# Norm statistics as columns, the convolution's norm inside the last heads, the output projection entered among them, two projection tiles opened side by side, and buffers placed at multiples of 128 bytes

## The reference

```python
for l in range(DEPTH):                                 # DEPTH = 2
    h = _rmsnorm(x, g_mix[l])                          # norm 0
    p = h @ w_in[l]
    c_q  = _rmsnorm(p[..., :384], g_q[l])              # norm 2
    c_kv = _rmsnorm(p[..., 384:640], g_kv[l])          # norm 1
    ...                                                # q, k, v of 8 heads, rotary parts
    y_attn = _mla_attention(q_nope, q_rope, k_nope, k_rope, v)
    a, gt = jnp.split(p[..., 672:], 2, axis=-1)
    u = _dwconv(a * jax.nn.sigmoid(gt), w_dw_conv[l], b_dw_conv[l])      # 31 taps, 512 channels
    u = jax.nn.silu(_layernorm(u, g_conv_ln[l], b_conv_ln[l]))           # norm 3
    x = x + jnp.concatenate([y_attn, u], axis=-1) @ w_o[l]
    h2 = _rmsnorm(x, g_ffn[l])                         # norm 4
    ...                                                # feed-forward
return _rmsnorm(x, g_final)
```

## Time and profile before

| what | value |
| --- | --- |
| median of three executions | 3025.68 us (3022.63 to 3028.54) |
| the profiled execution | 3028.47 us |
| its span, first to last instruction | 3026.7 us |
| mean granted TensorE clock | 0.965 of 2.4 GHz |
| busy: TensorE, VectorE, ScalarE, GpSimd | 93%, 59%, 26%, 58% |
| first mixer layer; second mixer layer | about 15 to 312 us; 675 to 957 us |
| second block | from about 1331 us |

### The profile page before, as it was taken

One profiled execution on the slowest core, in us unless ns is written; L12 is line 12 of the kernel. 1 busy time (PEld: TensorE's weight loads), 2 busy tenths in 40 slices (PEclk: granted clock), 3 DMA queues, 4 the chain that ended last, 5 costly groups with the idle time before them and its releaser, 6 DMA issues.

```text
span 3026.7 us, 35770 instructions
## 1 busy us (share of the span) xinstructions
PE 2827.2 (93%) x12832; PEld 2291.1 (76%) x12832; DVE 1775.7 (59%) x1941; ACT 777.0 (26%) x1256; POOL 1764.7 (58%) x1000
## 2 busy tenths in 40 slices
PE   6898899999787999989999989999999998899998
PEld 5676788887676888877776778888777777788876
DVE  8884566428855666256656557054666665842644
ACT  2332222102423222023555312011222221310202
POOL 5983566667944766654443447666553343566663
PEclk9998999999998999999999989999999998899999
DMA  3111222232011322322111113222221111232221
GB/s 134 56 43 49 77 97 97 99 104 91 28 36 55 110 95 95 106 79 73 63 63 56 63 65 108 93 95 97 77 90 62 56 56 50 76 99 96 97 98 49
DMA packets 66367, 237.36 MB, mean 78 GB/s; under 512 B 7152, under 2 KB 7408, under 8 KB 66224
## 3 DMA queue, kind: packets, MB, share of 16 engines
q1 hardware_dynamic: 65392, 234.00, 23.2%
q10 hardware_dynamic: 832, 1.51, 0.2%
HBM read 233.38 MB, written 2.10 MB: 78 GB/s over the span
## 4 chain that ended last, share of the span: by engine, by line
PE 77%; DVE 12%; DVEq 5%; issue 3%; ACT 2%; DMA 0%; ACTq 0%; SPq 0%
PE ps L457 23%; PE ps L463 22%; PE ps L460 22%; PE ps L1013 2%; PE ps L579 1%; DVE ps L1594 1%; DVE qw L2224 1%; PE ps L802 1%; DVEq L2226 1%; PE ps L1049 1%; PE ps L805 1%; DVE rstd L1567 1%; DVE ssum L1498 1%; DVE ssum L2072 0%; DVE x_lo L1486 0%
## 5 line engine op out<-in xcount | busy, mean ns | idle before, releaser
L398 POOL TENSOR_SCALAR w_hi<-w_raw 128x1024 fp32r<-128x1024 f32 x437 | 481.2, 1101 | 1193.3 <-PE ps L457 1182.5
L400 POOL TENSOR_TENSOR w_lo<-w_raw,w_hi 128x1024 fp32r<-128x1024 f32 x437 | 1108.8, 2537 | 36.4
L457 PE MATMUL ps<-x_hi,w_hi 128*128 128x512 f32 x2024 | 817.9, 404 | 74.1 <-DVE x_lo L2110 16.3
L463 PE MATMUL ps<-x_hi,w_lo 128*128 128x512 f32 x2024 | 797.8, 394 | 0.0
L460 PE MATMUL ps<-x_lo,w_hi 128*128 128x512 f32 x2024 | 797.8, 394 | 0.0
L457 PEld LDWEIGHTS ps<-x_hi,w_hi 128*128 128x128 f32 x2024 | 386.0, 191 | 177.0 <-issue 33.8
L460 PEld LDWEIGHTS ps<-x_lo,w_hi 128*128 128x128 f32 x2024 | 386.7, 191 | 83.5 <-issue 5.5
L463 PEld LDWEIGHTS ps<-x_hi,w_lo 128*128 128x128 f32 x2024 | 385.9, 191 | 82.9
L457 PE MATMUL ps<-a_hi,w_hi 128*128 128x512 f32 x512 | 201.8, 394 | 0.0
L463 PE MATMUL ps<-a_hi,w_lo 128*128 128x512 f32 x512 | 201.0, 393 | 0.0
L460 PE MATMUL ps<-a_lo,w_hi 128*128 128x512 f32 x512 | 199.2, 389 | 0.0
(11 more groups left out here) (377 smaller groups left out, 4566.6 us busy)
## 6 DMA issues: line engine op xcount, KB each, us to landing
w_raw<-wts SPq DMA_DIRECT2D x437, 512.0 KB, 3.3
xres<-xT SPq DMA_DIRECT2D x2, 1024.0 KB, 8.8
outT<-xres SPq DMA_DIRECT2D x1, 2048.0 KB, 7.1
pf<-pT ACTq DMA_DIRECT2D x2, 512.0 KB, 3.5
prm<-prm SPq DMA_DIRECT2D x1, 452.0 KB, 3.9
lev<-levels ACTq DMA_DIRECT2D x1, 384.0 KB, 3.1
wtmp<-pos SPq DMA_DIRECT2D x1, 128.0 KB, 3.1
ident<-identity SPq DMA_DIRECT2D x1, 64.0 KB, 10.6
```

The source lines that it names most:

```text
L398: nc.gpsimd.tensor_scalar(w_hi[:, s, :], w_raw[:, s, :], 1.0, 0.0, ALU.mult, ALU.add).then_inc(w_rounded[s], 1)
L400: nc.gpsimd.tensor_tensor(w_lo[:, s, :], w_raw[:, s, :], w_hi[:, s, :].bitcast(F32), ALU.subtract).then_inc(w_split[s], 1)
L457: mm = nc.tensor.matmul(out, whi, xhi, start=first, stop=False)
L463: return nc.tensor.matmul(out, wlo, xhi, start=False, stop=last)
```

## The change

1. **Norms in columns.** `row_stat` multiplies each 128x128 piece of the sum (as the stationary side) by a single column of ones, so the sums lie as 128 tokens by 4 columns. Root and reciprocal work on 128x4 (`rowm`). `row_factor` spreads the four columns again over 128 partitions with four products against the identity, into `ps[4]` or `ps[7]`, from where VectorE reads the factor. For norm 0 ScalarE copies it to `rstd`.
2. **Norms 1 and 2 without `rstd`.** ScalarE evacuates the five kv and q tiles itself, with the gain, and squares them from PSUM (`taken`). The missing division is undone by an epsilon that is scaled by the sum of squares of x (`ecol`, `ebias`; x's own sum now lies in `root`).
3. **Opening side by side.** `IN_STEPS` takes tiles 0 and 1 of the input projection alternately. The `row_stat` of norm 0 moves from behind tile 0 to behind kt = 4 of tile 2, its `row_factor` to before kt = 2 of tile 3. In the first layer GpSimd waits, before it splits block 2, until all of x is split.
4. **Convolution.** GpSimd takes channel tile 2 instead of 1, with `POOL_TAPS` {15: 3, 17: 4, 19: 24} instead of {10: 1, 11: 1, 12: 1, 13: 1, 15: 2, 17: 10, 18: 8, 19: 7}. VectorE's steps are placed anew: 45 instead of 39 before the keys.
5. **Key banks** [2, 3, 5, 1] instead of [2, 3, 0, 1], and output banks [1, 2, 3, 4, 0, 5, 1, 2].
6. **Last heads.** The sum of the four convolution tiles is made inside head 6, between the row maxima of the last head; the norm's sums, squares, root and scaling lie beside the last head; the output projection's first block begins before `weighted` of the last head (`mixed`).
7. **Places.** `ones_r`, `big` and `yconv` are moved so that every large buffer starts at a multiple of 128 bytes. Before, the buffers from `big` on started 64 bytes behind one (`f_hi`, `a_hi`, `xg_hi`, `y2_hi`, `k_hi`), those from `yconv` on 32 bytes (`u_hi`, `cq_hi`, `kv_hi`, `q_hi`). `x_hi`, `x_lo` and the weight ring were at a multiple of 128 already.
8. **Output** as eight DMAs, one behind each tile.

```diff
+IN_STEPS = ([(0, 0), (0, 1), (0, 2), (1, 0), (1, 1), (0, 3), (1, 2), (1, 3)]
+            + [(t, kt) for kt in range(4, KD) for t in (0, 1)] + [(t, kt) for t in range(2, W_IN) for kt in range(KD)])
...
+        top[0] = (top[0] + 127) // 128 * 128
         big = top[0]
...
-            sp.wait_ge(out_ready, KD)
-            sp.dma_start(out.rearrange("(t p) s -> p t s", p=P), xres[:, :, :]).then_inc(s_out, 16)
+            for m in range(KD):
+                sp.wait_ge(out_ready, m + 1)
+                sp.dma_start(x_out[:, m, :], xres[:, m, :]).then_inc(s_out, 16)
...
+                    if l == 0 and n == 2:
+                        pool.wait_ge(x_split, KD)
                     split(l * LBLK + n)
...
+            def row_stat(out, l, k, extra=None):
+                pe.wait_ge(sum_ready, l * 6 + (k + 1))
+                for tt in range(TT):
+                    c = slice(tt * P, (tt + 1) * P)
+                    mm = nc.tensor.matmul(out[:, tt:tt + 1], (root if k <= 0 else ssum)[:, c], ones[:, 0:1], start=True,
+                                          stop=extra is None)
+                    if extra is not None:
+                        mm = nc.tensor.matmul(out[:, tt:tt + 1], root[:, c], ecol[:, extra, :], start=False, stop=True)
+                mm.then_inc(stat_ready, 1)
+            def row_factor(out, n):
+                pe.wait_ge(root_used, n + 2)
+                for tt in range(TT):
+                    mm = nc.tensor.matmul(out[:, tt * P:(tt + 1) * P], rowm[:, 1, tt:tt + 1].to_broadcast([P, P]), ident[:, :],
+                                          start=True, stop=True)
+                mm.then_inc(factor_ready, 1)
...
+                last, wo = HEADS - 1, {}
+                stat(ps[6][:, :], l, 3)
+                for kt in range(TT):
+                    if kt == 0:
+                        weighted(last - 1, 0)
+                    scores(last, kt)
+                    if kt:
+                        weighted(last - 1, kt)
+                    if kt == 1:
+                        turned(last // 2 - 1)
+                wo[0] = block_in((lb, O_WO))
+                mixed(0, [0], [0, 1])
+                for qt in range(TT):
+                    weighted(last, qt)
+                row_stat(ps[7], l, 4)
+                mixed(0, [0], [2])
+                mixed(0, [1], [0, 1, 2])
+                row_factor(ps[7], l * 5 + 3)
+                turned(HEADS // 2 - 1)
...
+                for h in range(HEADS - 1):
+                    for qt in range(TT):
+                        if h == HEADS - 2 and qt == 2:
+                            conv(PER * 3)
+                            dve.drain()
+                            dve.wait_ge(stat_ready, l * 6 + 3)
+                            V.tensor_tensor(ssum[:, :], yconv[:, 0, :], yconv[:, 1, :], ALU.add)
+                        row_max(h + 1, qt)
+                        conv(1)
...
+                        if h == HEADS - 2 and qt == 2:
+                            dve.drain()
+                            V.tensor_tensor(ssum[:, :], ssum[:, :], yconv[:, 3, :], ALU.add)
+                            dve.drain()
+                            dve.wait_ge(pconv_done, l + 1)
+                            V.tensor_tensor(ssum[:, :], ssum[:, :], yconv[:, POOL_CH, :], ALU.add).then_inc(sum_ready, 1)
```

More of the change, by code:

```diff
@@ L479, in _ @@
                       + [b for b in W_O_BANK if b < 4] + [m % 4 for m in range(KD + 2 * FT)]):
                 BU[n] += 1
-            pe.wait_ge(s_id, 16)
             with pe.Fori(0, DEPTH) as l:
                 lb = l * (LBLK // R)
-                for t in range(W_IN):
+                entered = {}
+                for t, kt in IN_STEPS:
                     b = t % 4
[L488 to L492, removed]
-                        mm = three(ps[b][:, :], w_hi[:, s, kt * P:(kt + 1) * P], w_lo[:, s, kt * P:(kt + 1) * P],
-                                   x_hi[:, kt, :], x_lo[:, kt, :], kt == 0, kt == KD - 1)
+                    if kt == 0:
+                        bank(b, l * BU[b] + 1)
+                        entered[t] = block_in((lb, t))
+                    s = entered[t]
+                    if t < 2:
+                        pe.wait_ge(x_split, l * 2 * KD + (kt + 1))
+                    if t == 3 and kt == 2:
+                        pe.wait_ge(s_id, 16)
+                        row_factor(ps[4], l * 5)
+                    mm = three(ps[b][:, :], w_hi[:, s, kt * P:(kt + 1) * P], w_lo[:, s, kt * P:(kt + 1) * P],
+                               x_hi[:, kt, :], x_lo[:, kt, :], kt == 0, kt == KD - 1)
+                    if t == 2 and kt == 4:
+                        row_stat(ps[4], l, 0)
+                    if kt < KD - 1:
+                        continue
@@ L619, in _, with mixed @@
                             turned(h // 2 - 1)
-                    if h + 1 < HEADS:
-                        max_row(h + 1)
+                    max_row(h + 1)
                     if h + 2 < HEADS:
                         query(h + 2)
-                for qt in range(TT):
-                    weighted(HEADS - 1, qt)
-                turned(HEADS // 2 - 1)
-                for n, (half, m0) in enumerate(W_O_ORDER):
-                    s = block_in((lb, O_WO + n))
-                    ring = range(3) if n == 0 else range(4)
-                    for m, kts in [(m0, ring), (m0 + 1, ring)] + ([(m0, range(3, 4)), (m0 + 1, range(3, 4))] if n == 0 else []):
+                def mixed(n, ms, kts):
+                    half, m0 = W_O_ORDER[n]
+                    for m in ms:
                         b = W_O_BANK[m]
@@ L1487, in split_x, with add_square @@
                                        ALU.subtract).then_inc(x_split, 1)
-            def add_square(i, last, n, sums):
+            def add_square(i, last, n, sums, acc=ssum):
                 dve.drain()
@@ L1627, in _ @@
                 gate_a(1, 2)
-                conv(7)
+                conv(6)
                 gate_g(1, 3)
@@ L1795, in _, with residual @@
                                     ALU.subtract).then_inc(u_split, 1)
-                def residual(m, b, index, n, gain, sqn, sums):
+                def residual(m, b, index, n, gain, sqn, sums, total=ssum):
                     acc(index)
```

286 lines of the change are left out of this document (144 added, 142 removed).

## The result

The kernel after takes 2977.91 us (median of 4, 2976.41 to 2978.90), the one before 3027.11 (median of 4, 3022.63 to 3030.95): the ratio is 0.984, 95% interval [0.983, 0.986]. The prediction was 2977.5, in a range of 2948 to 2999. The total is right.

What follows compares the result with a forecast made beforehand. TensorE, busy 93%, bounds the kernel: time goes only where it waits, runs at 1.2 GHz or has slow products. 9.5 + 29 + 5.8 + 4.0 = 48.3 off 3028.5 gives 2980.2, 2.8 lower as median: 2977.5 us, range 2948 to 2999.

Steps and rivals of the forecast that it cites:

- Step 1: Large buffers at multiples of 128 bytes: their products take x's pace, saving 9.5 us (bounds 0 and 14).
- Step 2: Mixer opening: VectorE's evacuations start about 8 us later in the second layer; the first layer ends up like it.
- Step 3: Input projection: VectorE's saved work pays the opening back, about 3.5 us ahead when the heads begin (bounds 0 and 11).
- 2 ahead at the keys: VectorE in the input projection: net 10 us saved against 8 lost in the opening.
- Step 4: Head 6: VectorE waits some 3 us for GpSimd's channel, ending at 862.9; last head's lead is about 1.
- Step 5: Last head's scores to sum behind output projection: 67.3 us for 80.8; with the lead 14.5 a layer, 29 together.
- a sign of failure: Mixer tails: the forecast fails if drops to 1.2 GHz take over 12 us of each tail, or none.
- Step 6: Norm 4 and the final norm: 1.9 us saved twice and 2.0 at the end, 5.8 in all (2 to 7).
- Step 7: Output: the last piece of 256 KB lands in 3.1 to 3.9 us, saving 4.0 us (0 to 4.5).
- GpSimd is in time: Head 6: no stall for GpSimd's channel and no clock drop; up to 12 us a layer more, about 2957; chance 0.25.
- Two drops or an opening not paid back: Mixers: two full clock drops per tail, or VectorE's opening not repaid; 8 us a layer less, 2993; chance 0.13.
- Slower: Head 6: GpSimd's channel ends later, using up the gain at 24 us a layer; about 3047 if taps block; chance 0.03.

Runs made afterwards that it cites:

- experiment 1: Kernel before with only the buffer places changed to multiples of 128 bytes: 3015.87 us, ratio to before 0.9966.
- experiment 2: Kernel after with 32 bytes put ahead of its large buffers, u and yconv rounded up again: 2999.02 us, ratio to before 0.9910.
- experiment 7: Kernel after with input projection tiles 0 and 1 one after the other: 2975.20 us, ratio to before 0.9831.
- experiment 3: Kernel after with norm 0's row sums and factor spread five steps earlier: 2966.38 us, ratio to before 0.9800.
- experiment 4: Kernel after with VectorE's wait for GpSimd's channel and the convolution's mean moved later: 2968.55 us, ratio to before 0.9811.
- experiment 6: Kernel after with the output projection's first nine groups moved out of the last head to behind it: 2990.51 us, ratio to before 0.9885.
- experiment 9: Experiment 8's kernel with twelve more output projection products ahead of the last head's weighting, the spread later: 2960.06 us, ratio to before 0.9776.
- experiment 10: Experiment 8's kernel with GpSimd splitting block 16 ahead of its first three taps: 2957.86 us, ratio to before 0.9765.
- experiment 12: Kernel after with the edits of experiments 3, 4, 9, 10 and 11 together: 2965.57 us, ratio to before 0.9794.
- experiment 8: Kernel after with the edits of experiments 3 and 4 together: 2959.75 us, ratio to before 0.9790.
- experiment 11: Experiment 8's kernel without GpSimd's wait for the low halves of x in layer 1: 2961.84 us, ratio to before 0.9784.

## Why the prediction was right, and where it was not

**Step 1, places.** Right. 9.5 predicted, 10 to 11 measured alone (experiment 1). The mechanism holds in both directions (experiment 2). The Trainium skill (SBUF — State Buffer, Operand start alignment) asks for a multiple of the element size as a matter of legality and says that its runs timed nothing. Taken as a rule of speed it would have left this part at 0; the traces do not agree with that.

**Step 2, opening.** The lateness was right: 17.2 us behind the last addition in layer 2, as given. In layer 1 the sum comes 3.3 us later (34.0 before, 37.3 now, 4 predicted), by the two effects that were named: the low halves take 10.3 us for 16.0, the seven additions 14.1 for 5.4. The first evacuation comes 5.2 later, so this layer is better off than the second; the prediction made them equal. Between the first product and the first query it gained 6.9 us where layer 2 gained 1.3. Side by side does nothing for it (experiment 7). The trace shows one difference: in layer 1 TensorE stands for the sum in both kernels, before with 24 products done, now with 63, so that its 64th product starts 24.0 us behind the first and not 30.5. That this makes the 6.9 is not shown; experiment 3 puts the 64th back to 29.8, and its mixer is 3.0 us shorter all the same. The 0.2 us for the small reciprocal was read from records of TensorE, which say nothing of VectorE; that it took 0.18 is luck.

**Step 3, pay-back.** This step failed. "2 ahead at the keys" sums up VectorE's time and forgets when TensorE asks for it. At tile 6 VectorE is still behind; TensorE stands 3.7 us there and loses 4.45 more at the lower clock; the 14 tiles end at 92.0 us and not at 80.2. At the first query the lead is 1.3 us in layer 2, not 3.5. Experiment 3 starts the evacuations 3.6 us earlier and gains 11.5 us. By the end of head 6, just ahead of the stall of step 4, the lead of layer 2 has grown to 3.5 (186.8 against 190.3 behind the first product), so the price of this step is paid in the tiles, and of VectorE's lateness 1 us is left at the last head (step 4).

**Step 4, GpSimd's channel.** The mechanism was right and named in its place: VectorE stands in head 6, the last row maximum behind it, TensorE idle. The size was off, 7.7 for 3. Counted from the layer's first product the channel was to end at 187.3 and ended at 192.3: it began 3.3 later (86.7 for 83.4, the late opening again) and took 105.6 for 103.9. VectorE was at its wait at 185.4, predicted 184.4. The lead of 1 us at the last head became a lag of 6.3: the 7.7 us, and the products behind them at the lower clock until 852. Experiment 4 removes this stall; experiment 3 shows that an earlier norm does not.

**Step 5, tail.** Right in kind and too small. From the last head's first scores to the sum: 80.8 before, 60.0 after, where 67.3 was predicted, with 60.3 for the work alone. The 7 us for drops of the clock did not come; the only drop lies in the stall ahead of the head and just behind it, 1.6 us of it in this stretch (850.4 to 852). The prediction had named this as a sign of failure (drops over 12 us in each tail, or none), so its account of the clock here was wrong and only the waits were right. Experiment 6 gives a part of the reason: take the projection's products out of the head and the waits and the lower clock are back, 6.9 us in this layer. The other 14 of the 20.8 gained were not tested by a run that puts the norm back behind the head; for them stands the trace, in which TensorE is busy for 60.8 of 63.4 us. The error of step 4 and that of step 5 are of nearly one size, 7.3 each: layer 2 gained 14.5 up to the sum, to the tenth what was predicted, by luck (and with the 0.85 in it that step 1 had counted by itself). Layer 1 gained 20.4, by its better opening: 6.9 at the first query, where layer 2 had 1.3.

**Step 6, norms.** From the sum to the first product behind norm 4: 9.0 before, 8.2 in layer 2 and 7.4 in layer 1 after, so 0.8 and 1.6 and not 1.9 each. In layer 2 both sums and spread run at 1.2 GHz (the window's 0.50; 1.87 and 2.07 us), in layer 1 the spread alone (sums 1.05), and this is the 0.8 between the layers. The final norm gave the 1.9 (from the start of the last product ahead to that of the first behind, 11.6 and 9.7). 4.3 in all for 5.8.

**Step 7, output.** 5.0 for 4.0. The last piece of 256 KB lands in 2.0 us, not in the 3.1 of a smaller transfer at the start. Here the fixed cost of about 2 us in the Trainium skill (DMA: Bandwidth & Descriptors, Anatomy of one DMA — SWDGE (gpsimd) path) was nearer than the row I chose. It is fitted there to transfers that GpSimd issues, and these go by SyncE's queue; with the time for the data that stands beside it, 256 KB would take 2.6 us, an estimate, more than the 2.0 measured.

**The sum.** In span: mixers to the sum 20.4 + 14.5, norms 4.3, output 5.0, and outside the mixers 6.5 (feed-forward 1.2 + 1.5, second block 3.7): 50.7 of 50.8. These are stages of the same two traces, so that they must add up. That the 6.5 are the places is read from experiment 1, which gained 5.5 in these stages; its other 4.7 lay in the mixers (3.8 and 0.9), where step 1 had 1.7, within what one execution's stages are good to. The median was given as 2977.5 where the sum makes 2977.4.

**The rivals.** "GpSimd is in time" did not happen. "Two drops or an opening not paid back" happened in half: in the tiles of layer 2 the opening was not paid back, the drops in the tail stayed out. "Slower" was GpSimd's channel, and it was 5 late, not 24, and no run varied its end alone, so the price of one microsecond a layer is not shown. (The 34.6 of this rival should be 24 x 1.4 = 33.6; its chance does not hang on it.)

## What to carry to other kernels

A sum of an engine's saved time says nothing about when its results are asked for: put its own timeline against each place where the bound engine waits for it. A wait in a queue blocks all that stands behind it; ask what could be done first, and move it there (experiment 4), but expect the next dependency right behind the one you took away (experiments 9, 10 and 12). Where two chains start from the same point, an earlier start of both changes nothing between them (experiment 3); what is left to change is their lengths, or the place of the wait.

## What the runs showed of the hardware that I had not expected

- Moving 32 bytes changes the pace of products with 512 columns by 3%: 0.2267 us with the moving operand's tile at a multiple of 128 bytes, 0.229 at 64 behind one, 0.2335 at 32 behind one (experiments 1 and 2). The tiles a and f, 2592 products of the kernel, were moved. No run moved the weights or x.
- A wait of 3.7 us cost 8.1: 8.9 us at half the clock followed it (kernel after), and both went together (experiment 3). The 32 narrow products of `weighted` did not bring the clock down by themselves (1.00 in the window of the kernel after), with waits around them it stood at 0.77 (experiment 6).
- VectorE's addition of 0.69 us takes up to 2.6 beside GpSimd's splits, since it ends just behind the split (experiment 8). A gate that keeps GpSimd away from one stretch moved this price to the next one and saved nothing (experiment 11).
